# First sequence's x given channel by channel as well, its first norm on that layout, and its first two weight pairs multiplied directly by token half

## The reference, cut to what matters

```python
def rmsnorm(x, g):
    y = x * lax.rsqrt(jnp.mean(x * x, axis=-1, keepdims=True) + NORM_EPS) * g

h = rmsnorm(x, norm_mix[l])
z = h @ w_in[l]                      # 1024 x (512 pool + 3 * 768 attention) columns
...
q = partial_rope(q, pos); k = partial_rope(k, pos)
...
gates = jax.nn.sigmoid(h @ w_gate[l] + b_gate[l])
x = x + (g_a * a + g_b * b) @ w_out[l]
h = rmsnorm(x, norm_ffn[l])
x = x + (silu(h @ w_ffn_gate[l]) * (h @ w_ffn_up[l])) @ w_ffn_down[l]
```

## Time and profile before

| | us |
|---|---|
| median of three runs | 2514.36 (2513.21 to 2514.85) |
| span of the profiled execution, first to last instruction | 2511.7 |
| around the span (median less span) | 2.7 |
| TensorE (PE) busy | 2483.8, 99% of the span |
| GpSimd (POOL) busy | 1705.1, 68% |
| VectorE (DVE) busy | 1275.2, 51% |
| ScalarE (ACT) busy | 1030.4, 41% |
| first instruction on TensorE | 10.15 |
| first multiplication of pair 0, of pair 2 | 17.41, 73.41 |

### The profile page before, as it was taken

How to read it: one execution, slowest core, us unless ns; L and a number is a source line. 1 busy time by engine, 2 the same in 40 slices (tenths; PEclk the granted TensorE clock), 3 DMA queues, 4 the chain that set the end, 5 groups by cost and what they waited for, 6 DMA issues and landing times. The chain is left out here.

```text
span 2511.7 us, 33429 instructions
## 1 busy us (share of the span) xinstructions
PE 2483.8 (99%) x12124; PEld 2046.9 (81%) x12124; DVE 1275.2 (51%) x1753; ACT 1030.4 (41%) x2000; POOL 1705.1 (68%) x1268
## 2 busy tenths in 40 slices
PE   7999999999999999999999999999999999999998
PEld 6788878888888888888888887788888888888887
DVE  7753546654522222377988344456463222224768
ACT  5324553444433233346452345534453333333445
POOL 7676456544888888755687654573468888886544
PEclk9999999999999999999999999999999999999999
DMA  4544556472233333375453535655522333435644
GB/s 149 170 141 134 155 154 185 160 264 81 86 100 101 107 108 101 128 233 172 134 164 114 155 106 161 183 160 197 213 84 90 116 99 91 125 93 175 186 127 142
DMA packets 333090, 354.29 MB, mean 141 GB/s; under 512 B 38785, under 2 KB 240129, under 8 KB 331393
## 3 DMA queue, kind: packets, MB, share of 16 engines
q1 hardware_dynamic: 331488, 348.91, 44.3%
q10 hardware_dynamic: 1440, 3.25, 0.4%
HBM read 250.72 MB, written 101.38 MB: 140 GB/s over the span
## 5 line engine op out<-in xcount | busy, mean ns | idle before, releaser
L1233 PE MATMUL ps<-S,t_hi 128*128 128x512 f32 (+1 forms) x2328 | 914.8, 393 | 5.2 <-DVE S L2196 2.1
L1235 PE MATMUL ps<-S,t_lo 128*128 128x512 f32 (+1 forms) x2328 | 903.0, 388 | 0.0
L1234 PE MATMUL ps<-S,t_hi 128*128 128x512 f32 (+1 forms) x2328 | 902.1, 387 | 0.0
L1233 PEld LDWEIGHTS ps<-S,t_hi 128*128 128x128 f32 x2328 | 437.8, 188 | 99.5 <-issue 8.5
L1235 PEld LDWEIGHTS ps<-S,t_lo 128*128 128x128 f32 x2328 | 437.8, 188 | 90.0
L1234 PEld LDWEIGHTS ps<-S,t_hi 128*128 128x128 f32 x2328 | 438.2, 188 | 86.3 <-issue 1.0
L1005 POOL TENSOR_TENSOR t_lo<-wraw,t_hi 128x512 fp32r<-128x512 f32 x185 | 248.1, 1342 | 205.1 <-ACT t_hi L1750 202.2
L1005 POOL TENSOR_TENSOR t_lo<-wraw_ff,t_hi 128x512 fp32r<-128x512 f32 x225 | 289.3, 1287 | 78.7 <-ACT t_hi L1750 69.5
L1005 POOL TENSOR_TENSOR t_lo<-R,t_hi 128x512 fp32r<-128x512 f32 x154 | 217.9, 1419 | 177.9 <-ACT t_hi L1750 177.9
L1750 ACT CAST t_hi<-wraw_ff 128x512 fp32r<-128x512 f32 x225 | 139.9, 623 | 364.2 <-PE ps L1235 362.9
L1233 PE MATMUL ps<-t_hi,d_hi 128*128 128x512 f32 x616 | 240.6, 391 | 0.3 <-POOL t_lo L1005 0.3
(11 more groups left out here) (185 smaller groups left out, 3881.7 us busy)
## 6 DMA issues: line engine op xcount, KB each, us to landing
d_raw<-d_rows SPq DMA_DIRECT2D x154, 256.0 KB, 2.9
d_rows<-act_f SPq DMA_DIRECT2D x110, 256.0 KB, 2.1
wraw_ff<-w_ffn_up SPq DMA_DIRECT2D x44, 512.0 KB, 4.7
R<-w_ffn_down SPq DMA_DIRECT2D x88, 256.0 KB, 3.1
wraw<-w_in SPq DMA_DIRECT2D x42, 512.0 KB, 5.8
sp_rows<-gst SPq DMA_DIRECT2D x80, 256.0 KB, 2.4
wraw_ff<-w_ffn_gate SPq DMA_DIRECT2D x40, 512.0 KB, 5.1
wo_raw<-w_out SPq DMA_DIRECT2D x36, 512.0 KB, 4.2
```

What stands on the lines that cost most here:

```text
L1233: nc.tensor.matmul(o_ps, w[0], r[0], start=begins, stop=False, skip_group_check=True)
L1234: nc.tensor.matmul(o_ps, w[0], r[1], start=False, stop=False, skip_group_check=True)
L1235: return nc.tensor.matmul(o_ps, w[1], r[0], start=False, stop=ends, skip_group_check=True)
```

## The change

A second copy of the first sequence's x, turned on the host (`xt`, channels by tokens), and the gain as a column per channel block (`gmix`) are given to the kernel. For the first sequence:

- The low token half of x is loaded as `HT[0]` (four loads of two channel blocks by 512 tokens). Each token's sum of squares now runs down the partitions: ACT squares eight blocks (`square_channels`), TensorE adds them with 32 plain float32 matmuls of two columns against a tile of ones (`squared_sums`), behind ten matmuls of that tile with itself. The square roots are spread over a tile, turned by four transposes (`factor_rows`) and multiplied in by DVE, block by block (`channel_norms`). For the high half the sums come from x by tokens as before (`square_tokens`), the data from `xt`.
- The 28 groups of four transposes of the first sequence are gone. High and low parts are made straight from `HT`, both in SBUF.
- Pairs 0 and 1 are multiplied plainly: four times `direct_half(n, h)` (pair n, token half h), 48 matmuls each, 192 in place of 168. Their weight sums and result sums fall away. Their eight operands have buffers of their own (`extra_hi`, `extra_lo` for pair 1).
- `S1` to `S4` of x are needed from pair 2 on. They are made on POOL and DVE meanwhile, 1024 elements a row at a time (`open_sums`, `open_thirds`, `open_lows`).
- `FOLD_TR` is 24, and the loads are issued in another order.
- For the second sequence nothing moves.

```diff
-FOLD_TR = 14
+FOLD_TR = 24
...
-OPENING = (0, 2, 7, 9, 1, 4, 3, 5, 6, 8, 10, 11, 12, 13)
...
+DIRECT = 14
+OPEN_COUNT = (1, 2, 3, 4, 5, 6, 7, DIRECT)
+HALF_DONE = ((1, 3), (2, DIRECT))
...
+POOL_OPEN = [("A11", 3), ("A12", 1), ("A21", 2), ("A21", 3), ("A22", 1), ("A22", 3)]
+DVE_OPEN = [key for key in OPEN_HIS if key not in POOL_OPEN]
...
+WARM = 10
...
+            def squared_sums():
+
+                pe.wait_ge(ones_set, 1)
+                for _ in range(WARM):
+                    nc.tensor.matmul(ps[:, 5, 0:P], ones[:, :], ones[:, :], start=True, stop=True)
+                for k in range(KD):
+                    pe.wait_ge(ssx_ready, k + 1)
+                    for p in range(4):
+                        ins = nc.tensor.matmul(ps[:, 4, 2 * p:2 * p + 2], squared[k][:, p * P:(p + 1) * P], ones[:, 0:2],
+                                               start=k == 0 and p == 0, stop=k == KD - 1, skip_group_check=True)
+                ins.then_inc(tr_full, 1)
+
+            def factor_rows(h):
+
+                pe.wait_ge(spread_ready, h + 1)
+                for p in range(4):
+                    ins = nc.tensor.transpose(ps[:, 2 + h, p * P:(p + 1) * P], spread[h][:, p, :], ident_sb[:, :])
+                ins.then_inc(tr_full, 1)
+
+            def direct_half(n, h):
+
+                for k in range(KD):
+                    c, kk = divmod(k, 4)
+                    part = f"A{h + 1}{c + 1}"
+                    if n == 0:
+                        open_ready(pe, part, kk)
+                    for j in range(2):
+                        b = OPEN_BANKS[n][OPEN_ORDER[2 * h + (j if h == 0 else j)]]
+                        if h == 0 and kk == 0:
+                            pe.wait_ge(t_ready, OPEN_COUNT[4 * n + 2 * c + j])
+                        if k == 0:
+                            bank_read(b)
+                        w = [a[:, kk * P:(kk + 1) * P] for a in operand_of(n, 2 * c + j)]
+                        ins = three(ps[:, b, :], w, [S[:, :, KIND[part], hl, kk, :] for hl in range(2)], k == 0, k == KD - 1)
+                ins.then_inc(prod_done, DIRECT - 3 if n and h else 1)
+
+            def opening():
+
+                squared_sums()
+                pe.wait_ge(ident_in, 16)
+                factor_rows(0)
+                direct_half(0, 0)
+                factor_rows(1)
+                direct_half(1, 0)
+                last[0], last[1] = ("rope_read", 0, 1), ("rope_read", 0, 2)
+                direct_half(0, 1)
+                pe.wait_ge(xn_ready, 2 * KD)
+                direct_half(1, 1)
...
+            def channel_norms(h, ks):
...
+                    x = HT[h][k // 2][:, k % 2, :]
+                    V_.scalar_tensor_tensor(out=x, in0=x, scalar=gain_c[:, k:k + 1], in1=ps[:, 2 + h, :], op0=ALU.mult, op1=ALU.mult
+                                            ).then_inc(xn_ready, 1)
...
+            def open_lows(keys):
+
+                for part, k in keys:
+                    src, ks = open_source(part, k)
+                    dve.wait_ge(shi_ready, HI_AT[part, k])
+                    n = KIND[part]
+                    V_.tensor_tensor(S[:, :, n, 1, ks, :], src, S[:, :, n, 0, ks, :].bitcast(F32), ALU.subtract
+                                     ).then_inc(s_ready, 1)
...
+                    elif part == "S3":
+                        act.wait_ge(third_made, k + 1)
+                        for key in HIGH_KS + [("S1", 0), ("S1", 1)]:
+                            open_ready(act, *key)
...
+                open_his(HIGH_KS)
+                open_his(OPEN_HIS[16:18])
+                operand_hi(0, DIRECT)
+                operand_hi(0, DIRECT + 1)
+                open_his(OPEN_HIS[18:20])
+                operand_hi(0, DIRECT + 2)
+                operand_hi(0, DIRECT + 3)
+                open_his(OPEN_HIS[20:])
```

More of the change, by code:

```diff
@@ L171 @@
[L171 to L182, removed]
@@ new lines, in encoder @@
+        HT = [[at(f"ht{h}_{p}", o, [2, H2]) for p, o in enumerate(os)] for h, os in enumerate(ht_at)]
+        squared = [at(f"squared{k}", XR + 16384 + 2048 * k, [H2]) for k in range(KD)]
+        x_high = [at(f"x_high{p}", SP_ * p + 4096, [D]) for p in range(4)]
+        squares0 = [at(f"squares0_{p}", o, [D]) for p, o in enumerate((16384, 3 * SP_ + 16384, 24576, SP_ + 24576))]
+        spread = [at(f"spread{h}", SP_ + 16384 + 2048 * h, [4, P]) for h in range(2)]
+        ones = at("ones", 2 * SP_ + 16384, [P])
@@ L1098, in pair_parts @@
                     first_sums(s, (n - FF0) // 2 - 1)
[L1099 removed]
+                if n != FF0:
                     low_part(s, 7 * n + 4, t1[:, :, :])
@@ new lines, in opening @@
+            def opening():
+                direct_low(0, 0)
+                direct_low(0, 1)
+                direct_low(0, 2)
+                direct_low(0, 3)
+                open_low("A11", 3)
+                open_low("A12", 1)
+                for q in range(4):
+                    direct_low(1, q)
+                open_low("A21", 2)
+                open_low("A21", 3)
+                open_low("A22", 1)
+                open_low("A22", 3)
+                for part in ("S1", "S2"):
+                    for i in range(2):
+                        open_sums(part, i)
+                first_pair_sum(0, 2)
+                second_pair_sum(0, 2)
+                leading_lows(0, 2, (0, 1))
+                third_pair_sum(0, 2)
+                for i in range(2):
+                    open_sums("S4", i)
+                leading_lows(0, 2, (2, 3))
@@ L1180, in _ @@
                     leading_lows(s, 0, (2, 3))
-                for n in range(0 if s else 1, FF0):
+                for n in range(0 if s else 2, FF0):
                     pair_parts(s, n)
@@ L1287, in parts_ready @@
                 if n == 0:
-                    pe.wait_ge(s_ready, due("s_ready", s, max(PART_AT[s][part, p] for p in range(pairs)) + 1))
+                    pe.wait_ge(s_ready, due("s_ready", s, max(PART_AT[part, p] for p in range(pairs)) + 1))
                     return
@@ L1447, in pair_product @@
                     scores(s, 2 * q + 1)
-                pe.wait_ge(t_ready, due("t_ready", s, place(s, m) + 1))
-                if n in (0, FF0):
+                pe.wait_ge(t_ready, due("t_ready", s, m + 1))
+                if s == 0 and n == 2:
+                    for k in range(4 if part[0] == "A" else 2):
+                        open_ready(pe, part, k)
+                elif n in (0, FF0):
                     parts_ready(s, n, part, 4)
@@ new lines, in opening @@
+            def opening():
+                squared_sums()
[8 more added lines that the diff above has]
+                direct_half(1, 1)
+                for b, job in ((6, 3), (7, 4), (0, 5), (1, 6), (2, 7), (3, 8)):
+                    last[b] = ("rope_read", 0, job)
```

583 lines of the change are left out of this document (305 added, 278 removed).

## The result

The changed kernel takes 2520.34 us (median of 7 runs, 2519.58 to 2522.63), the kernel before 2513.33 (7 runs, 2512.67 to 2514.85). The ratio is 1.0029, 95% interval 1.0019 to 1.0039: slower by 7.0 us. The profiled execution took 2521.4, 1.8 more than its span of 2519.6. In every timed execution whose span is on record, of all kernels here, the time is 1.7 to 2.2 above the span, so the 2.7 "around the span" of the kernel before is about 0.9 too much: it compared a span with the median of other executions.

A forecast was written before the change was run, and what follows sets the result against it. TensorE was taken to bound the kernel, only its opening able to gain. Queue delays at product 21, +4.8 to +5.5, plus 0.7 for the clock gave +6.0: span 2517.7, plus 2.7, 2520.4 us; 8-in-10 range 2509 to 2527.

The forecast's parts named there:

- the 2.7 "around the span": Whole execution: 2.7 us added to the forecast span of 2517.7 to give the time, 2520.4.
- VectorE's queue: Ahead of product 19: VectorE's work from 55.6 delivers `v` at 91.3, or 82.9 with nothing in its way.
- The start: Opening of the first sequence: first multiplication at 18.4 against 17.41 before, so nothing gained there.
- one of the prediction's own signs of being wrong: Opening: the prediction would be wrong if the sums took over 10 us.
- the half-clock rival: Opening: sums at half clock to their end, first multiplication 24.0, product 21 at +11, 2525.4 us; chance 0.25.
- The idle time of 2.4 near 31: Behind half (0,0): TensorE idles some 2.4 us until pair 1's operands are ready at 33.2.
- 92.46 + 6.0 - 18.4: Way to product 21: its start before, 92.46, plus 6.0 forecast delay, less first multiplication at 18.4.
- ScalarE's copy: Product 16: waits for the bank 0 copy queued behind casts of `S3` and `S4`, a gap of 7.5 us.
- 0.84, 8.4 in all: VectorE ahead of product 19: ten long two-SBUF-operand operations beside GpSimd each cost 0.84 us extra, 8.4 in all.
- The second gap: Ahead of product 19: TensorE waits 4.4 us for VectorE's `v`.
- The clock behind the gap: After the gaps near 31 and 75: half clock adds only 0.7 us, since VectorE's queue leads.
- The side computation: Its pieces only move, from behind product 14 to behind product 24; no cost counted.

The follow-up runs named there:

- e11: Changed kernel without the ten matmuls of the ones ahead of the sums; 2521.91 us, ratio 1.0036.
- e6: Changed kernel with the squared blocks first added on VectorE, and TensorE kept at work by 36 ones matmuls instead of 10, plus 5 and 9 more; 2516.39 us.
- e1: Changed kernel with ScalarE's copy of bank 0 for pair 2 moved ahead of the casts of S3 and S4; 2524.33 us, ratio 1.0048.
- e4: Changed kernel with VectorE's eight low parts and two differences reading one operand from PSUM, a stand-in with other numbers; 2514.14 us, ratio 1.0004.
- e9: e8 plus ScalarE copying each sum into PSUM for VectorE's low parts, and casting operands of products 18 and 19 ahead of S4; 2510.24 us.
- e8: Changed kernel with e7's order, the additions on VectorE and the filled TensorE of e6 together; 2515.39 us, ratio 1.0010.
- e10: e8 plus 18 matmuls of the identity into bank 7 ahead of product 16's wait; 2515.46 us, ratio 1.0009.
- e12: Kernel before with only the side computation's pieces moved from behind product 14 to behind 24; 2513.13 us beside 2512.78, ratio 1.0002.
- e5: Changed kernel with the eight squared blocks first added on VectorE, so TensorE sums with 8 passes instead of 64; 2518.06 us, ratio 1.0019.
- e7: e3 with the third sum of pair 2 also ahead of its first rotation, behind the low parts of S4; 2519.47 us, ratio 1.0028.
- e3: Changed kernel with both reorderings at once, e1's on ScalarE and e2's on VectorE; 2523.65 us, ratio 1.0046.
- e2: Changed kernel with only VectorE reordered: u, v of pair 2 and low parts of S3 moved earlier; 2526.57 us, ratio 1.0059.

## Why the prediction was right, and which of its steps were not

The sign was right, and so was the main cause: VectorE's queue, made long by operations with two tensors in SBUF beside GpSimd. That the time, 2520.4, was met to 0.1 us is luck. The start came 3.8 us later than worked out (22.21 for 18.4), and the way from there to product 21 was 2.9 shorter (77.17 for 92.46 + 6.0 - 18.4 = 80.06). The rest cancelled too: 1.0 more behind product 21, 0.9 too much counted around the span, and a profiled execution 1.1 above the median.

- **The start** was wrong, and one of the prediction's own signs of being wrong came true: the sums took over 10 us (11.97). "I take 13.9: the ten matmuls of ones lie ahead" put the end of the sums at 13.9; they ended at 17.5. The inference from 17.41 in the kernel before was the error: a clock that had risen behind 128-column transposes says nothing of one that must hold through passes of two columns. The clock was full from 4.2 to 7.6 only, and without the ten it isn't full at any time in the sums (e11). So the first multiplication came at 22.21, not 18.4, between forecast and the half-clock rival (24.0). From it to product 14 the 48 us stood as worked out (66.4 - 18.4 = 48.0). The idle time of 2.4 near 31 didn't appear, since half (0,0), at half clock for its first six microseconds, took 13.7 us instead of 12.0 and filled it; at full clock (e6) it took 12.5, and TensorE idled 1.0 and 0.5 us behind it.
- **The rival's price was wrong too**: with the first multiplication at 24.0 it gave +11 at product 21; where it came at 24.02 (e11), product 21 is at 101.06, +8.6. The laid-out queues were too pessimistic behind 60 us.
- **ScalarE's copy**: a wait of 7.5 was forecast and 7.51 measured, four microseconds later than forecast. The mechanism (casts of `S3` and `S4` ahead of it, those waiting for `S1`'s low parts) is in the rows. That this wait by itself is what costs the time fell with e1: three queues end within a few us of each other there, and undoing one shows the next.
- **VectorE's queue**: `v` was forecast at 91.3 and ended at 93.67, with the half (0,1) ahead of it 3.7 late; so VectorE's stretch was 1.3 us shorter than counted. Most of that is the term "0.84, 8.4 in all", which was 7.4 (1.95 us each instead of 1.21). The second gap, forecast 4.4, was 0.76: product 16 came 3.9 us later than forecast and took 1.4 longer at half clock, `v` only 2.4 later. That the two SBUF operands are the cause, and that they decide between slower and level, is shown by e4; e9, with the right numbers in place, agrees. By the rule named in the prediction, the Trainium skill's "exclusive lock" (SBUF — State Buffer, section "SBUF: two separate sides"), one operation waits for the whole of the other. The traces agree: one low part took 3.37 us and another 1.21, and an even split of the port would, by an estimate from these rows, at most double the 1.21 to 2.42.
- **The clock behind the gap**: 0.7 was added; product 16 took 87.45 - 83.30 = 4.15 instead of 2.72, 1.4 more. As argued, the row that leads takes it back: in the order of e8, filling the gap won nothing (e10). In the changed kernel's own order it wasn't tried.
- **The side computation** only moves: e12 shows it for the kernel before.

So the loss comes from three things. The start, which the sums' many passes cost: 2.3 us by the medians (e5), 3.95 with the clock kept full as well (e6). VectorE's and GpSimd's operations in each other's way: 6.2 us by the medians, 7.1 in the profile (e4). And an order with the sums of pair 2 at the end of VectorE's queue: 0.9 by the medians, 2.1 from the first multiplication on (e7). Against them stand the 8.0 us that TensorE gains between its first multiplication and product 14.

The medians of e5, e7 and e8 show less than product 21 does in their profiles, and most of it is in the choice of the profiled execution: set against its own time instead of the median, e7 is 3.4 us below the changed kernel's profiled execution, as product 21 is (3.4), e8 6.7 (7.3) and e5 3.3 (4.1). The start itself varies between executions of one kernel. In the profiles where the clock was full for a while ahead of the multiplications, the mean granted clock of the execution is 0.993 to 0.995; in those with ten or no matmuls of the ones where it wasn't (e1, e4, e11), with the first multiplication near 24, it is 0.997 to 0.999. Of the 51 timed executions with ten such matmuls (the changed kernel, e1 to e5, e7) 12 have 0.997 or more, and they are among the slowest of their kernel: the changed kernel's two took 2521.69 and 2522.63, the median of its other five is 2520.10, and e11, late in all executions, has 2521.91. That the clock wasn't full ahead of the multiplications in these 12 is read from the mean alone; only two of them (e1's and e4's) were profiled. What decides it from one execution to the next stays open.

## What to carry to other kernels

When work is taken off the engine that bounds, read which engine is left without a pause in the same stretch (here VectorE, 39.38 of 40 us): there its work and its order count, and moving one wait uncovers the next queue (e1). An operation that begins to read both tensors from SBUF while GpSimd runs costs both engines, so it is worth trying to let an idle engine put one operand in PSUM (e9, where an order changed with it). Sums across partitions cost TensorE by the number of passes (64 took 12 us, 8 took 1.9), so add the blocks on an idle engine first. And set a profile beside the time of its own execution, not beside the median.

## What the runs showed of the hardware

- The 64 passes of two columns took 10.71 (twice), 11.18, 11.97, 13.80 and 13.81 us in six profiles of the same instructions (e3 and e7, e2, after, e4, e1), 0.11 us a pass at 2.4 GHz and 0.215 at 1.2. In the first four the clock was full for a while behind the ten matmuls (from 4.2 to 7.6 us, after) and fell again during the sums, in the last two it wasn't full ahead of 26 us. That alone moves the start by 3.1 us between executions. With 36 matmuls ahead, and the additions in place of 56 of the passes, it stayed full (e6).
- The window's clock column prints 1.00 ahead of the first record; the length of a pass is the surer reading (0.21 against 0.11 us).
- GpSimd's low parts of 512 elements take 1.31 us beside VectorE operations with one operand in PSUM and 2.27 beside such with two in SBUF; VectorE's of 1024 take 1.21 and up to 3.37.
